# Gathering each expert's rows inside the expert ahead of it, with 18 weight buffers instead of 14

## The reference

```python
def swiglu(h, w1, w3, w2):
    return (jax.nn.silu(h @ w1) * (h @ w3)) @ w2

def moe_swiglu(h, w_router, w1, w3, w2):
    logits = jnp.einsum('bsd,de->bse', h, w_router).astype(jnp.float32)
    top_val, top_idx = lax.top_k(logits, TOP_K)
    top_w = jax.nn.softmax(top_val, axis=-1)
    gates = jnp.sum(jax.nn.one_hot(top_idx, N_EXPERTS, dtype=jnp.float32) * top_w[..., None], axis=-2)
    out = jnp.zeros_like(h)
    for e in range(N_EXPERTS):
        out = out + gates[..., e:e + 1].astype(h.dtype) * swiglu(h, w1[e], w3[e], w2[e])
    return out
```

## Time and profile before

| | us |
|---|---|
| three runs | 1340.5, 1344.78, 1345.29 |
| median | 1344.78 |
| the profiled execution's own time | 1340.57 |
| its span, from the first to the last instruction | 1338.7 |
| TensorE busy in the span | 1287.4 |
| VectorE, ScalarE busy | 372.0, 245.3 |

### The profile page before, as it was taken

How to read it: one execution, slowest core, us unless ns; L and a number is a source line. 1 busy time by engine, 2 the same in 40 slices (tenths; PEclk the granted TensorE clock), 3 DMA queues, 4 the chain that set the end, 5 groups by cost and what they waited for, 6 DMA issues and landing times.

```text
span 1338.7 us, 30672 instructions
## 1 busy us (share of the span) xinstructions
PE 1287.4 (96%) x13725; PEld 755.5 (56%) x13725; DVE 372.0 (28%) x486; ACT 245.3 (18%) x318; POOL 21.4 (2%) x37
## 2 busy tenths in 40 slices
PE   9999999999999999999899999999999999999774
PEld 7998888888998843543333543443453353354222
DVE  5767644436466540010010110002001011001002
ACT  5644433324652210000000000000000000000001
POOL 2000000000000000000000000000000000000000
PEclk9999999999999799999999999999999999999998
DMA  9825755513834579999999999999999999999995
GB/s 312 304 83 193 261 185 179 183 33 128 292 127 187 238 270 394 407 408 408 402 409 409 401 408 408 391 408 409 401 401 408 408 388 408 409 392 408 408 392 210
DMA packets 140256, 430.74 MB, mean 322 GB/s; under 512 B 12375, under 2 KB 18807, under 8 KB 140002
## 3 DMA queue, kind: packets, MB, share of 16 engines
q1 hardware_dynamic: 138546, 423.49, 81.8%
q0 software_dynamic: 1584, 5.33, 1.1%
HBM read 427.71 MB, written 2.11 MB: 321 GB/s over the span
## 4 chain that ended last, share of the span: by engine, by line
PE 86%; DMA 10%; DVE 2%; issue 1%; ACT 1%; SPq 0%; POOL 0%; POOLq 0%; DVEq 0%
PE psum L1834 35%; PE psum L1854 17%; DMA ring<-in_moe_w 10%; PE psum L1363 9%; PE psum L1365 9%; PE psum L1364 9%; PE psum L1579 1%; PE psum L1790 1%; PE psum L1888 1%; PE psum L1382 0%; PE psum L1715 0%; PE psum L1538 0%; DVE h L887 0%; PE psum L1539 0%; SPq L474 0%
## 5 line engine op out<-in xcount | busy, mean ns | idle before, releaser
L1834 PE MATMUL psum<-ring,xe 128*32 128x512 f32 (+1 forms) x5440 | 520.9, 538 | 19.7 <-DMA ring<-in_moe_w 19.7
L1834 PEld LDWEIGHTS psum<-ring,xe 128*32 128x32 f32 x5440 | 173.8, 110 | 347.2 <-issue 269.7
L1854 PE MATMUL psum<-ring,gT 128*32 128x256 f32 x4864 | 271.2, 380 | 12.0 <-DMA ring<-in_moe_w 12.0
L1854 PEld LDWEIGHTS psum<-ring,gT 128*32 128x32 f32 x4864 | 159.2, 110 | 129.2 <-issue 19.6
L1221 DVE TENSOR_TENSOR gate<-gate,psum 128x768 f32<-128x768 f32 (+3 forms) x32 | 25.4, 795 | 531.9 <-ACT gate L785 531.9
L869 DVE TENSOR_TENSOR wlo<-raw,whi 128x2048 fp32r<-128x2048 f32 (+1 forms) x66 | 145.3, 2227 | 56.9 <-ACT whi L617 56.9
L785 ACT ACTIVATE gate<-psum 128x768 f32<-128x768 f32 (+3 forms) x32 | 21.9, 684 | 636.0 <-PE psum L1834 636.0
L617 ACT CAST whi<-raw 128x2048 fp32r<-128x2048 f32 (+1 forms) x66 | 120.5, 1861 | 58.1 <-PE psum L1365 32.5
L1363 PE MATMUL psum<-whi,f_hi 128*128 128x512 f32 (+1 forms) x320 | 123.8, 387 | 1.9 <-DVE wlo L869 0.9
L1365 PE MATMUL psum<-whi,f_lo 128*128 128x512 f32 (+1 forms) x320 | 121.4, 379 | 0.0
L1364 PE MATMUL psum<-wlo,f_hi 128*128 128x512 f32 (+1 forms) x320 | 121.3, 379 | 0.0
(11 more groups left out here) (246 smaller groups left out, 820.2 us busy)
## 6 DMA issues: line engine op xcount, KB each, us to landing
ring<-in_moe_w SPq DMA_DIRECT2D x672, 512.0 KB, 12.5
raw<-in_ffn_w SPq DMA_DIRECT2D x33, 1024.0 KB, 5.5
raw<-in_w_mix_in SPq DMA_DIRECT2D x21, 1024.0 KB, 7.4
raw<-in_w_mix_out SPq DMA_DIRECT2D x8, 1024.0 KB, 5.0
raw<-in_w_mix_in SPq DMA_DIRECT2D x4, 544.0 KB, 5.9
x<-in_x SPq DMA_DIRECT2D x2, 512.0 KB, 4.2
raw<-in_w_mix_in SPq DMA_DIRECT2D x2, 512.0 KB, 6.5
bias_by_distance<-bias_once POOLq DMA_DIRECT2D x1, 1024.0 KB, 7.7
```

What stands on the lines that cost most here:

```text
L1834: ins = mm(banks(j, n)[o:o + 32, g, 0:2 * q].rearrange("p (i b c) -> p i b c", i=2, c=64), rows_[:, k * CAP + 32 * g:k * CAP + 32 * (g + 1 ...
L1854: ins = mm(bank[bk][32 * q:32 * (q + 1), at_:at_ + 256], gT[j % 2][:, a:a + 32], w[:, o:o + 256], start=j == 0 and n == 0 and at_ == 0, st ...
```

## The change

Rows are gathered expert by expert. `gather(v)` makes the rows of one expert only: 32 matmuls of 96 columns, into two banks, copied straight into `xe` by ScalarE and VectorE, half each. The first expert's gather stays behind the routing; the gather for each later expert stands in TensorE's list between the last `e_up` of the expert ahead and its third `e_down`. VectorE makes the 0/1 matrix of the next expert (`pick_rows`) and the diagonals of this one (`spread_places`) after the first quarter's product. `turn_places(v)` spreads one expert's places by one matmul of 256 columns behind the gather, and `picks_turned` compares straight out of the bank. `xe_all`, `place_rows` and the large `pick` and `diag` are gone, and in their place the ring has 18 buffers for the first sweep. A later sweep, which runs only when an expert overflows its slots, keeps 14 (`RING_MORE`). SP's loop over the experts of the first sweep is written out.

```diff
-RING = 14
+RING = 18
+RING_MORE = 14
...
-        ring_at += [w_at[i % 2] + 8192 * (1 + i // 2) for i in range(10)] + [w_at[0]]
+        ring_at += [w_at[i % 2] + 8192 * (1 + i // 2) for i in range(10)] + w_at
+        ring_at += [ffn_arena + 8192 * i for i in range(RING - 15)]
...
+        def ring_slot(f):
+
+            return f % RING if f < PER_SWEEP else (f - PER_SWEEP) % RING_MORE
...
-                slot = f % RING
+                slot = ring_slot(f)
                 if f < RING and slot < RAW_FIXED:
                     sp.wait_ge(lo_ready, MOE0 - RAW_FIXED + slot + 1)
+                elif f < 15:
+                    sp.wait_ge(block_used, min(MOE0, MOE0 - SLOTS + 1 + (slot - RAW_FIXED) // 2))
                 elif f < RING:
-                    sp.wait_ge(block_used, MOE0 - SLOTS + 1 + (slot - RAW_FIXED) // 2)
-                return ring[slot], sp.lower_val(PER_EXPERT * turn + (f + 1))
+                    sp.wait_ge(go_ps, 4)
+                room = 1 if f < PER_SWEEP else 1 + RING - min(RING_MORE, PER_SWEEP % RING)
+                return ring[slot], sp.lower_val(PER_EXPERT * turn + (f + room))
...
+            def gathered(v):
+                act.wait_ge(xe_ps, 2 * v + 1)
+                nc.scalar.copy(xe[:, 0:4 * CAP], bank[0][:, 0:4 * CAP]).then_inc(xe_act, 1)
...
+            def pick_rows(who):
+                for t in range(NT):
+                    ins = nc.vector.tensor_scalar(pick[:, CAP * t:CAP * (t + 1)], consts[:, K_IOTA:K_IOTA + CAP],
+                                                  place1[:, ds(who + EXPERTS * t, 1)], None, ALU.is_equal)
+                ins.then_inc(pick_sb, 1)
+
+            def gathered(v):
+                dve.wait_ge(xe_ps, 2 * v + 2)
+                nc.vector.tensor_copy(xe[:, 4 * CAP:8 * CAP], bank[1][:, 0:4 * CAP]).then_inc(xe_dve, 1)
...
-                picks(0)
+                pick_rows(0)
                 rest(xn_lo[:, D:2 * D], h[:, D:2 * D], xn_hi[:, D:2 * D], xn_h, 2, xn_ready)
                 nc.vector.tensor_copy(counts, bank[5][:, 16:24]).then_inc(counts_sb, 1)
-                picks(1)
-                gathered(0, 0)
...
+                nc.vector.tensor_copy(ones_r[:], ones[:])
+                gathered(0)
...
+            def spread_places(who):
+                for t in range(NT):
+                    ins = nc.vector.tensor_scalar(diag[:, P * t:P * (t + 1)], ident(),
+                                                  place1[:, ds(who + EXPERTS * t, 1)], None, ALU.mult)
+                ins.then_inc(diag_sb, 1)
...
                 mult(sweep, 0, e, turn)
-                picks_turned(sweep, who, e, turn)
+                spread_places(who)
+                if not last:
+                    pick_rows(chosen_expert(turn + (e + 1)))
                 for j in range(1, STEPS):
                     mult(sweep, j, e, turn)
                 if not last:
-                    then = chosen_expert(turn + (e + 1))
-                    dve.wait_ge(moe_used, blocks_done(sweep, PER_EXPERT * e + 27, turn))
-                    n = KD * CAP
-                    nc.vector.tensor_copy(xe[:], xe_all[:, ds(n * then, n)]).then_inc(xe_sb, 1)
+                    gathered(v + 1)
+                picks_turned(sweep, e, v)
...
+            def gather(v):
+
+                def part(k, xn, t, start, stop):
                     a = t * D + k * P
+                    return mm(bank[k // 4][:, k % 4 * CAP:(k % 4 + 1) * CAP], xn[:, a:a + P],
+                              pick[:, CAP * t:CAP * (t + 1)], start=start, stop=stop, skip_group_check=True)
+
+                pe.wait_ge(pick_sb, v + 1)
+                for k in range(KD):
+                    for t in range(NT):
+                        part(k, xn_hi, t, k % 4 == 0 and t == 0, False)
+                pe.wait_ge(xn_ready, 2)
+                for k in range(KD):
+                    for t in range(NT):
+                        ins = part(k, xn_lo, t, False, k % 4 == 3 and t == NT - 1)
+                    if k % 4 == 3:
                         ins.then_inc(xe_ps, 1)
...
+            def turn_places(v):
+
+                pe.wait_ge(diag_sb, v + 1)
+                mm(bank[2][:, 0:SEQ], ones_r[:], diag[:], start=True, stop=True).then_inc(rows_ps, 1)
...
                 e_up(3, f + 24, turn, xe, range(0, 4), n)
+                pe.wait_ge(e_gT, STEPS * turn + (STEPS * (EXPERTS * sweep + e) + 3))
+                if not last:
+                    gather(v + 1)
+                turn_places(v)
                 e_down(sweep, 2, f + 28, e, turn, n)
...
-                    pe.wait_ge(xe_sb, v + 2)
+                    pe.wait_ge(xe_act, v + 2)
+                    pe.wait_ge(xe_dve, v + 2)
+                    pe.wait_ge(pickT_sb, v + 1)
                     e_up(0, f + 32, turn, xe, range(0, 4), then)
```

More of the change, by code:

```diff
@@ L378, in down_place, with fills @@
             return (6 + g, 0) if n == LIGHT else (6 + g // 2, 256 * (g % 2))
[L380 to L386, removed]
+        def ring_slot(f):
+            return f % RING if f < PER_SWEEP else (f - PER_SWEEP) % RING_MORE
+        def fills(f):
+            if f < PER_SWEEP:
+                return f // RING + 1
+            first = -(-(PER_SWEEP - ring_slot(f)) // RING)
+            return first + (f - PER_SWEEP) // RING_MORE + 1
         def hidden(engine, c, t, i, turn):
@@ L501, in sweep_experts @@
                 expert(sweep, 0, 0)
-                with sp.Fori(0, EXPERTS - 2) as e:
-                    expert(sweep, 1, chosen_expert(e + 1), turn=e)
+                if sweep == 0:
+                    for e in range(1, EXPERTS - 1):
+                        expert(sweep, e, chosen_expert(e))
+                else:
+                    with sp.Fori(0, EXPERTS - 2) as e:
+                        expert(sweep, 1, chosen_expert(e + 1), turn=e)
                 expert(sweep, EXPERTS - 1, chosen_expert(EXPERTS - 1), last=True)
@@ L802, in sweep_experts @@
             def sweep_experts(sweep):
[L803 to L806, removed]
+                gathered(EXPERTS * sweep)
                 expert(sweep, 0)
@@ L1227, in mult, with picks_turned @@
                 ins.then_inc(e_gT, 1)
[L1229 to L1232 removed]
+            def spread_places(who):
[3 more added lines that the diff above has]
+                ins.then_inc(diag_sb, 1)
+            def picks_turned(sweep, e, v):
+                dve.wait_ge(rows_ps, v + 1)
                 for g in range(groups(sweep, e)):
[L1234 to L1235 removed]
+                    ins = nc.vector.tensor_scalar(pickT[:, SEQ * g:SEQ * (g + 1)], bank[2][:, 0:SEQ],
+                                                  consts[:, K_SLOT + g:K_SLOT + g + 1], None, ALU.is_equal)
                 ins.then_inc(pickT_sb, 1)
@@ L1285, in sweep_experts @@
                              nc.vector.tensor_scalar(to, to, -float(CAP), None, ALU.add))
-                    slots = consts[:, K_SLOT:K_SLOT + GROUPS]
-                    link(nc.vector.tensor_scalar(slots, slots, float(CAP), None, ALU.add))
-                    slots = first_slot[:, 0:GROUPS]
-                    link(nc.vector.tensor_scalar(slots, slots, float(32 * LIGHT if sweep == 1 else CAP), None, ALU.add))
-                    for half in range(2):
-                        picks(half)
-                    for half in range(2):
-                        gathered(sweep, half)
-                    first_rows(sweep)
+                    pick_rows(0)
+                    gathered(EXPERTS * sweep)
                 expert(sweep, 0)
@@ L1811, in turn_places @@
-            def turn_places():
-                pe.wait_ge(diag_sb, 1 + 4)
-                for i in range(4):
-                    mm(bank[3 + i], ones_r[:], diag[:, 512 * i:512 * (i + 1)], start=True, stop=True)\
-                        .then_inc(rows_ps, 1)
+                    return mm(bank[k // 4][:, k % 4 * CAP:(k % 4 + 1) * CAP], xn[:, a:a + P],
+                              pick[:, CAP * t:CAP * (t + 1)], start=start, stop=stop, skip_group_check=True)
+                pe.wait_ge(pick_sb, v + 1)
@@ L1845, in e_down @@
                 for n in range(tiles):
-                    w = ring[(f + n // 2) % RING]
+                    w = ring[ring_slot(f + n // 2)]
                     if n % 2 == 0:
```

100 lines of the change are left out of this document (20 added, 80 removed).

## The result

The changed kernel took 1332.55 us (median of four runs, 1329.12 to 1333.77), the kernel before 1345.03 us beside it. The ratio is 0.991, 95% interval [0.9882, 0.9939]. In a later series of five runs it took 1331.79 us, ratio 0.9923 [0.9908, 0.9938]. The forecast was 1333, in a range of 1325 to 1341, on the side "faster by over 0.5%". Of the 19 executions of the kernel before in the first series of experiments, five took 1340.5 to 1342.3 us at a mean granted clock of 0.993 to 0.995, and fourteen 1343.0 to 1346.0 us at 0.989 to 0.993; by its time, 1340.57 us, the profiled one lies with the five.

What follows compares the result with a forecast made beforehand. Transfers were taken to set the end, gaining 4.1 (start) + 10.3 (ring) + 1.1 (slot-spreading matmuls moved out of the first expert) - 3.9 (inner gather) = 11.6 us; 1344.8 - 11.6 = 1333 us, range 1325 to 1341.

Steps and rivals of the forecast that it cites:

- What bounds the kernel: Expert stage: transfers hardly ever rest after 477 us, and the last of them sets the end.
- The start, 4.1 us: Ahead of the first expert: shorter compares and gather begin expert matmuls 6.8 us early, less 2.7 us for the clock.
- the dear gather: Rival on the gathers: 0.177 us a matmul despite 96 columns; 6 to 10 us gained, 1337 us; chance 0.18.
- The 2.7 of the forecast: First expert: TensorE's clock rises only after 5.4 us of expert matmuls, half of that, 2.7 us, being lost.
- The ring, 10.3 us: Before and in the first expert: four more buffers fill the transfers' silence, so transfers start 10.3 us sooner.
- the buffers buy nothing: Rival on the ring: four early blocks are not sent in the silence; 1.3 us remain, 1343.5 us; chance 0.10.
- about 17 of 18: Between the light experts: the transfers gain on TensorE until about 17 of 18 buffers are taken, which just fits.
- The inner gather, -3.9: Inside seven experts: each gather adds 3.9 us to TensorE; the first delays the full ring's buffers once.
- The gathers stop the clock: Rival on inner gathers: each brings the clock down and costs 9.9 us; 20 us over, 1365 us; chance 0.07.
- three signs of being wrong: Gather steps of 0.177 us or more, TensorE's clock falling inside an expert, or TensorE at the end with all blocks landed.
- break-even of 7.1 us: Inner gathers: cost per gather at which TensorE's summed work passes the old end of the transfers.
- TensorE's slack, 11 us: At the end: TensorE would be ready for the last block at 1300.7 us, the transfers 11 us later.

Runs made afterwards that it cites:

- the wide one: Changed kernel with only the first gather moving 224 columns per matmul instead of 96: 1329.37 us; with inner gathers also in four pieces: 1329.82 us.
- late filling: Changed kernel with 18 buffers, but the four new ones filled only once the first buffer has come back: 1338.29 us, ratio 0.9966.
- The doubled wide gathers: Changed kernel with each of the seven inner gathers done twice, each matmul moving 224 columns instead of 96: 1345.99 us, ratio 1.0009.
- the single wide kernel: Changed kernel with inner gathers done once, each matmul moving 224 columns instead of 96: 1331.73 us, ratio 0.9919.
- in pieces: Changed kernel with each inner gather cut into four pieces, one ahead of each block of the third w2 chunk: 1332.76 us; doubled, 1350.41 us.

## Why the prediction held, step by step

**What bounds the kernel: right.** The transfers set the end. 14, 16 and 18 buffers show it, and so does the kernel with hardly any inner gathers, where some 24 us less of TensorE's work is worth about one gather.

**The start, 4.1 us: 4.9, and 4.3 in the second profile.** The 20.60 us piece came 526.28 - 521.94 = 4.3 us earlier, 6.0 with the offset of this execution, of which 1.1 is the moved `turn_places`. The gather began at 461.09 - 1.7 = 459.4 us, 0.6 later than I had it (the last small matmuls of the routing ahead of it already ended at 460.04 - 1.7 = 458.3 us, where they had ended at 457.75), and cost 7.03 us (6.9 predicted); the near end, 0.112 for 96 columns, was the right one (0.116 measured), the dear gather is refuted. The clock came back at 471.6 us, 2.8 us after the first ring matmul began and not 5.4, so half of that, 1.4, was lost instead of 2.7. The steps partly cancel. This one term is not settled by one profile: in the eleven profiles with a narrow first gather the clock came back 2.7 to 5.2 us behind the first ring matmul, and the first chunk took 42.72 to 43.94 us against 41.41 in both with the wide one, so 1.3 to 2.5 us were lost. The 2.7 of the forecast is a little over the top of that. That the narrow gather keeps the clock down was right, and the wide one shows its price, 2 to 3 us.

**The ring, 10.3 us: about 10 by the trace, 8 to 10 by the runs.** The last transfer landed near 1313.4 us, 1311.7 without the offset, which is the predicted time; in the second profile of the changed kernel, which has no such offset, the landing ends at 1311.19:

```profile
1294.94 16.25 DMA ring<-in_moe_w
1311.33 4.98 PE psum L1855 x64
```

Before, it ended at 1307.29 + 15.88 = 1323.17. So the transfers gained 1323.17 - 1311.7 = 11.5 us, and 11.5 - 4.9 - 1.1 + 4.4 = 9.9 is left for the ring. The second profile gives nearly the same: 12.0 us at the landing, 526.28 - 520.91 - 1.1 = 4.3 at the start, 3.3 for the gather, 12.0 - 4.3 - 1.1 + 3.3 = 9.9. What is left is an estimate, since the loss at the gather is one. The rival "the buffers buy nothing" would have been the 14-buffer kernel; it forecast 1343.5 and that kernel took 1341.78.

The ring also had the room that the forecast asked for, "about 17 of 18". SP's transfers of the changed kernel until 1218 us:

```profile
L471 SPq DMA_DIRECT2D ring<-in_moe_w x414: 327/940/5337, 388.2 to 1217.8; - x138
L481 SPq DMA_DIRECT2D ring<-in_moe_w x196: 327/916/3452, 447.4 to 1198.3; - x196
```

610 halves are 305 blocks, and the gather at 1218.47 us stands behind block 288 (8 + 6 x 42 + 28): 17 are taken.

**The inner gather, -3.9: right as work; the transfers lost 3.3 by it, 4.4 with the clock.** A full expert without a fall grew by 4.02 us, one with a fall by 5.6. The first one counts in the sum because the ring is full there, the windows at 564 us show it. That a kernel whose ring is not full at that moment escapes this delay I had not seen; it is why late filling cost only 5.8 us.

**"The gathers stop the clock": the mechanism is there, its price was not.** A clock that falls inside an expert was one of the three signs of being wrong that I had named, and it came. I had set it at all seven gathers and 9.9 us each. The changed kernel has it behind two to four, and since the fall comes at the gather's end it costs 12.18 - 10.50 = 1.7 us, 5.6 with the gather. My break-even of 7.1 us was the one against the old end of the transfers. Against their new end the 11 us of slack, spread over seven gathers, put it at 3.9 + 11 / 7 = 5.5 us, so seven falls would just have used up the slack. That it was only two to four is chance (12 falls in 42), and the forecast had no such term: a small piece of luck. The Trainium skill (TensorE: Matmul & The Clock Gate, "HAM oscillation — how this bites in real kernels") explains such falls by waits for data in which TensorE idles between short bursts. Here they come with TensorE busy 4.00 us of 4.00, so the rows go further than the page: the clock of a busy engine that moves few columns falls too. The fall of before at 451.1 us came with TensorE at work as well. Ahead of it the engine was busy 10.49 us of 11.00, from 448.80 us on with the router's matmuls of 8 columns:

```profile
440.00:451.00 11.00, 10.49 (x77) 9.30 (x75) 5.21 (x8) 3.30 (x6) 1.15 (x2) 1.00 1.03 409
```

**TensorE's slack, 11 us: right, and it paid for the clock.** (The forecast's sum of TensorE's work is 1.1 us too low: with 1.73 us a block as written it is 808.7 us and not 807.6, which leaves 10 us.) The doubled wide gathers make TensorE the bound, with no fall: span 1345.5. Each is 7.34 - 3.76 = 3.6 us longer than a single wide one, together 25; without them TensorE would end at 1320, and the single wide kernel's span is 1331.5, so 11 us of slack. Four falls take 6.8 of it. This is why taking the falls away, in pieces or by width, changed nothing (1332.76 and 1331.73 against 1331.79), and why doubling them did: past the break-even each microsecond a gather counts seven times.

**The end: not in the sum, and the hit is partly luck.** The last piece took 5.38 us (4.98 in the second profile) instead of 3.69 in the earlier trace rows, at a clock of 0.69; the few TensorE matmuls in the last wait (1.93 us busy of 5.50) are much the same as before, where the clock stayed up:

```profile
1317.50:1323.00 5.50, 2.07 (x36) 0.94 (x32) 0.00 (x0) 0.00 (x0) 0.00 (x0) 1.00 0.41 165
```

Behind VectorE's last instruction the changed kernel's span goes on for 5.1 us in both profiles (from 1327.16 to 1332.3 in the first), where it had 3.5 before (1335.20 to 1338.7). I had carried the old tail over, so 3.3 us are missing from the sum for the span, 2.9 by the second profile. With them and the offset of 1.7 the forecast span of 1327.1 becomes the measured 1332.3, to 0.2 us. The median was hit all the same, because I had set the forecast 4.2 us above the profile: the execution shown of before stood so far under its median, and the changed kernel's stood 1.2 above its own. The longer executions of before have the lower mean clock; whether they lose it in the last piece, as the changed kernel does, no profile shows. Nine of the ten profiles of variants in which a transfer sets the end have a fall of the clock there; the one with 16 buffers has none. Why it falls in that wait, and why the tail is longer, was not tried.

## What to carry to other kernels

Find the resource that never rests after some point, then look for the last silence ahead of it: buffers filled in that silence are worth nearly their transfer time, here 2 to 2.5 us for each megabyte, though in the steady stage half the ring looks unused. Work put on the engine that doesn't set the end is free up to its slack, so work out the break-even per repetition against the end that the change itself will set (5.5 us a gather here) and let an experiment double the cost to see where it lies. Where each matmul comes with a fresh 128x128 stationary, 96 columns took as long as 224 here, and in a long run they cost the clock: let such matmuls carry more columns, or spread them between other work.

## What the runs showed of the hardware that was not expected

- A matmul with a fresh 128x128 stationary takes 0.116 us with 96 columns and 0.115 to 0.118 with 224 (32 in 3.76 us, 64 in 7.34).
- TensorE's clock fell to half while TensorE was busy throughout. Gathers of 96 columns: with 32 matmuls, 3.7 us, 12 falls in 42; with 64, 7 in 7. In pieces of 0.8 to 1.9 us, with w2 matmuls between them: none at 21 gathers. With 224 columns: none in 14.
- A fall at a gather of 3.7 us lasted 3.4 us, at one of doubled length 10.2 us.
- Going from 32-column to 128-column stationaries and back costs about 0.1 us each way (2.73 instead of 2.59 us for a block, 1.02 instead of 0.93 for a piece of gather).
